# One 128-row bias load from a 128-copy table in place of two 64-row loads from a 64-copy table

## The chip, the cores and the metric

The kernel runs on one core of one Trainium2 chip. The metric is the device time of that core in microseconds. Three runs of the kernel before gave 2240.4, 2241.33 and 2242.48 us; their median is 2241.33 us. The lower the time, the better.

The engines have these names here: PE is TensorE, DVE VectorE, ACT ScalarE, POOL GpSimd, SP SyncE. PE multiplies, DVE and ACT prepare operands and post-process, POOL does small elementwise work and issues some DMAs, SP issues the weight loads.

## The reference

The program is a small transformer stack on 256 tokens with model width 1024. Two mixer layers come first; each adds to x the output projection of three gated attention branches. Then come four layers of a second block (sliding-window, gated-linear, forgetting and again sliding-window attention, each with a SwiGLU). All is float32. The part that matters here is the relative-position bias of two of the three branches of a mixer layer:

```
bias = bias_tab[t5_bucket(kpos[None, :] - qpos[:, None])]        # diff_attention, 8 heads
s = einsum('bqmhd,bkmhd->bmhqk', qblk, k) * scale + bias

bias = bias_tab[t5_bucket(delta * r)]                            # dilated_group, 3 groups of 4 heads
s = einsum('bnqhd,bnkhd->bnhqk', qs, kb) * scale + bias
s = where(valid, s, NEG_INF)
```

The bias of a query q and a key k depends on the head and on k - q alone. There are 8 + 12 = 20 heads with such a bias, and the kernel folds the mask of the dilated groups into it. Both mixer layers use the same table.

## The kernel before

**Weights.** Every weight matrix is streamed from HBM in pieces of 256 rows by 512 columns (512 KB, one DMA or two of 256 KB) into eight buffers `raw`. SP issues these loads (`h_piece`); a buffer is loaded again when DVE has read its last piece. A piece is then split into a rounded part `whi` (ACT, L144) and a rest `wlo` (DVE, L150), of which there are seven buffers each, and PE multiplies three times: high by high, high by low, low by high (L138). Some pieces (`in_ada_w`) are not multiplied on PE but reduced on DVE into a block of the tile `pool` (L155, then L158).

**Order of the work.** Every engine's program is recorded by one planner, which walks the network once and sends each step to the engine that owns it. Engines run their lists in order and wait for each other by semaphores. Small steps are placed by `soon`, a list that counts GEMM steps down; the attention heads are placed between weight pieces by estimated costs. The planner's estimates have no term for the bias loads or for the writes of the table.

**The bias.** Early on (`table`, L1077 on) one small matmul and one DVE addition (`h_btab`) make a block `btb` of 20 rows by 512 columns: row h holds the bias of head h as a function of k - q, for -255 to 256. To turn such a row into a tile in which partition q holds the row shifted by q, it is copied through HBM. `write_scratch(k)`, k = 0 to 3, is called 4, 7, 10 and 13 steps after the start of the first GEMM; each call issues one DMA on POOL's queue that writes every row of `btb` 16 times into the HBM tensor `bias_scratch`, which so holds 64 copies of each row. When the four writes have landed, `btb`'s two blocks of `pool` are free again; the next to use them is DVE's accumulation of an `in_ada_w` piece.

`get_bias(u)` is called for each attention unit: once per head of the differential branch, and for three heads of a dilated unit. It takes one of six buffers `bias_t` [128, 384] and issues, on POOL's queue, two DMAs (`h_bias`): partitions 0 to 63 and partitions 64 to 127. The source steps 511 elements from one partition to the next in copies that are 512 long, so that each partition starts one element earlier; the second half starts 64 elements earlier in the first copy. Both wait for the four writes and for the buffer's last reader. The reader is DVE's L158 `S<-A,bias_t` (`h_dil` and `h_diff`, step "max"), which adds the scaled logits in PSUM to the bias. In all there are 20 such tiles in each of the two mixer layers.

**POOL's list.** Beside these it holds the write and the reading back of one layer's memory keys and values (`kv_scratch`), and the small powers of the norms (`sm<-sm,mhalf`, L150), one of 128x1 or 128x2.

Of the kernel before, what the change touches and what calls it, by code (L numbers as in the profile page):

```python
# [7 lines left out]
F32 = mybir.dt.float32  # L8
# [5 lines left out]
P = 128  # L14
# [74 lines left out]
class Tally:  # L89
# [3 lines left out]
    def __init__(self, nc, ctx):  # L93
        self.nc, self.ctx, self.sem, self.n, self.value, self.real = nc, ctx, {}, {}, {}, False
# [164 lines left out]
class Memory:  # L259


    def __init__(self, nc, ctx, I, C, out):
        def sb(name, shape, dt=F32):
            return ctx.enter_context(nc.sbuf_tensor(name, shape, dt))

        self.I, self.C, self.out = I, C, out
        self.raw = sb("raw", [P, NRAW, 2, 512])
        self.whi = sb("whi", [P, NSPL, 2, 512], F32R)
        self.wlo = sb("wlo", [P, NSPL, 2, 512], F32R)
        self.X = sb("X", [P, 2, D])  # L270
        self.HTh, self.HTl = sb("HTh", [P, 8, T], F32R), sb("HTl", [P, 8, T], F32R)
        self.OTh, self.OTl = sb("OTh", [P, 8, T], F32R), sb("OTl", [P, 8, T], F32R)
        self.pool = sb("pool", [P, NB, 256])
        self.bias_t = sb("bias_t", [P, 6, 384])
        self.ident = sb("ident_t", [P, P])
        self.identr, self.maskr = sb("identr", [P, P], F32R), sb("maskr", [P, 256], F32R)
        self.cols = sb("cols", [P, 80])
        self.adb = sb("adb", [P, 192])
        self.mod = sb("mod", [P, 256])
        self.sm = sb("sm", [P, SM])  # L280
        self.c8 = sb("c8", [P, 8])
        self.ones = sb("ones", [P, 1])
        self.mhalf = sb("mhalf", [P, 16])
        self.nlam = sb("nlam", [P, 2])
        self.rmem = sb("rmem", [P, 2])
        self.w16 = sb("w16", [P, 256], F32R)
        self.w16h, self.w16l = (self.w16[:, 128 * i:128 * i + 128].rearrange("p (c n) -> p c n", n=16) for i in range(2))
        self.sel = sb("sel", [P, 16], F32R)
        self.S = [sb(f"S{j}", [P, 1040]) for j in range(2)]
        self.W = [sb(f"W{j}", [P, 1536]) for j in range(2)]  # L290
        self.GB = [ctx.enter_context(nc.psum_tensor(f"G{i}", [P, 512], F32)) for i in range(4)]
        self.AB = [ctx.enter_context(nc.psum_tensor(f"A{i}", [P, 2, 512], F32)) for i in range(2)]
        self.kvs = nc.dram_tensor("kv_scratch", (2, P, D), F32, kind="Internal").ap()
        self.mrows = nc.dram_tensor("mod_rows", (4, 64, P), F32, kind="Internal").ap()
        self.scratch = nc.dram_tensor("bias_scratch", (20, 64, 512), F32, kind="Internal").ap()


def cseg(w, r0, nk, segs):
# [128 lines left out]
class Order:  # L427
# [661 lines left out]

    def write_scratch(self, k):  # L1090

        self.scr.append(self.load("POOL", f"scr{k}", self.M.scratch[:, 16 * k:16 * k + 16, :],
                                  self.btb.a[0:20, :].unsqueeze(1).to_broadcast([20, 16, 512]), [self.tbt, self.step]))
        if k == 3:
            self.btb.release(self.scr)

    def get_bias(self, u):
        u["bias"] = []
        for i, h in enumerate([u["h"]] if u.kind == "diff" else [8 + gi * 4 + u["h"] for gi in range(3)]):
            r = self.bias_at.pop(0)  # L1100
            evs = [(f"bias{r}", (u.name, i, k)) for k in range(2)]
            for k in range(2):
                src = bass.AP(self.M.scratch.tensor, h * 64 * 512 + 127 - 64 * k, [[511, 64], [1, 384]])
                self.h_bias(r, 64 * k, src, self.scr, self.bias_free[r], evs[k])
            u["bias"].append((r, evs[1]))

    def biased(self, u):

# [2089 lines left out]
class GpSimdE(Order):  # L3198
# [26 lines left out]
        e.wait_ge(*self.at(prev))  # L3225
        e.tensor_tensor(m, m, gq, ALU.add).then_inc(*self.up(added))

    def h_bias(self, r, p, src, scr, free, ev):
        e = self.e
        for t in scr + free:  # L3230
            e.wait_ge(*self.at(t))
        e.dma_start(self.M.bias_t[p:p + 64, r, :], src).then_inc(*self.up(ev, 16))

    def h_rope(self, ps, t, dst, nh, tmp, cb, full, trp, free, read, done):
        e = self.e
# [79 lines left out]
```

## Time and profile before

| | |
|---|---|
| Median of the runs | 2241.33 us (2240.4 to 2242.48) |
| Time of the profiled execution | 2242.48 us |
| Span in its trace | 2240.7 us |
| PE busy / weight loads on PE | 2158.3 us (96%) / 1926.5 us (86%) |
| DVE / ACT / POOL busy | 1565.2 / 1029.2 / 206.1 us |
| Bytes moved | 472.98 MB, of these 29.61 MB on POOL's queue |

A span is the time from the first to the last instruction of the trace; the profiled execution's own time is 1.8 us longer. Busy time of PE says how long it had a matmul under way. The chain that ended last is followed back from the last instruction, at each step to whatever released it; what is not on it did not set the end in this execution. A timeline row shows a start, a duration, an instruction and, in brackets, how long the engine was idle before and what ended that. A DMA has two times: the issue, during which POOL is occupied, and the landing, counted from the start of the issue.

### The profile page before, as it was taken

How to read it: one execution, taken by the hardware profiler on the slowest of the kernel's cores; microseconds unless marked ns; L12 is line 12 of the kernel's file. 1: busy time of each engine (PE TensorE's matmuls, PEld its weight loads, DVE VectorE, ACT ScalarE, POOL GpSimd, SP SyncE). 2: the span in 40 equal slices, each digit the busy share in tenths (PEclk: the TensorE clock that was granted, in tenths of full speed). 3: DMA queues.
4: the chain of work that ended last, by engine and by line, in shares of the span. 5: the costliest groups of instructions: out<-in, count | busy, mean ns of one | idle time of the engine just before them, and what ended most of it. 6: DMA issues, size and time to landing. Idle time of an engine off the chain costs nothing.

```text
span 2240.7 us, 34043 instructions
## 1 busy us (share of the span) xinstructions
PE 2158.3 (96%) x13827; PEld 1926.5 (86%) x13827; DVE 1565.2 (70%) x2153; ACT 1029.2 (46%) x1698; POOL 206.1 (9%) x244
## 2 busy tenths in 40 slices
PE   7999999999999999999999998999999999999996
PEld 6999888889998888777999787999898899788996
DVE  6577657766676677667898677899645895667454
ACT  5444445544444564455434544444455443454342
POOL 1101001101010011010001001001000001111010
PEclk9999999999999999999999999999999999999998
DMA  8977645577786455534899434799544797425551
GB/s 303 290 249 218 226 156 161 168 235 225 240 266 199 135 165 200 190 122 143 301 343 343 155 107 141 262 358 357 186 132 141 262 355 247 148 94 187 189 181 64
DMA packets 297425, 472.98 MB, mean 211 GB/s; under 512 B 20257, under 2 KB 153067, under 8 KB 297269
## 3 DMA queue, kind: packets, MB, share of 16 engines
q1 hardware_dynamic: 286708, 441.20, 58.4%
q0 software_dynamic: 10560, 29.61, 4.4%
q8 instruction: 109, 1.79, 0.3%
q14 instruction: 48, 0.39, 0.1%
HBM read 465.88 MB, written 4.85 MB: 210 GB/s over the span
## 4 chain that ended last, share of the span: by engine, by line
PE 88%; DVE 6%; issue 2%; ACT 2%; POOL 1%; DMA 1%; SPq 0%; DVEq 0%; POOLq 0%; ACTq 0%
PE G L138 69%; PE A L138 16%; PE G L141 2%; DVE pool L158 2%; DVE wlo L150 1%; DVE pool L150 1%; POOL sm L150 1%; ACT pool L144 1%; DVE X L150 1%; PE A L141 1%; DVE HTl L158 0%; DMA raw<-in_w_mem_kv 0%; ACT HTh L144 0%; DVE sm L155 0%; DMA pool<-mod_rows 0%
## 5 line engine op out<-in xcount | busy, mean ns | idle before, releaser
L150 DVE TENSOR_TENSOR wlo<-raw,whi 128x1024 fp32r<-128x1024 f32 x640 | 772.7, 1235 | 181.2 <-ACT whi L144 179.5
L144 ACT ACTIVATE whi<-raw 128x1024 fp32r<-128x1024 f32 x640 | 646.5, 1054 | 192.9 <-DMA raw<-in_ffn_w_gu 94.8
L138 PE MATMUL G<-HTh,whi 128*128 128x256 f32 x2336 | 672.8, 288 | 9.6 <-ACT pool L144 4.8
L138 PE MATMUL G<-HTh,wlo 128*128 128x256 f32 x2336 | 662.3, 284 | 0.0
L138 PE MATMUL G<-HTl,whi 128*128 128x256 f32 x2336 | 662.2, 283 | 0.0
L138 PEld LDWEIGHTS G<-HTh,whi 128*128 128x128 f32 x2336 | 449.3, 192 | 17.9 <-DVE wlo L150 9.4
L138 PEld LDWEIGHTS G<-HTl,whi 128*128 128x128 f32 x2336 | 449.5, 192 | 2.1
L138 PEld LDWEIGHTS G<-HTh,wlo 128*128 128x128 f32 x2336 | 449.1, 192 | 0.0
L144 ACT ACTIVATE pool<-G 128x512 f32<-128x512 f32 (+2 forms) x208 | 115.5, 573 | 537.9 <-PE G L138 503.8
L138 PE MATMUL G<-whi,HTh 128*128 128x512 f32 (+1 forms) x784 | 313.4, 400 | 14.9 <-ACT HTh L144 9.3
L138 PE MATMUL G<-whi,HTl 128*128 128x512 f32 (+1 forms) x784 | 304.2, 388 | 4.3 <-DVE HTl L158 4.1
L138 PE MATMUL G<-wlo,HTh 128*128 128x512 f32 (+1 forms) x784 | 301.9, 385 | 0.0
L158 DVE SCALAR_TENSOR_TENSOR pool<-raw,c,pool 128x512 f32<-128x512 f32 x336 | 267.7, 797 | 7.4
L158 DVE SCALAR_TENSOR_TENSOR pool<-pool,G 128x512 f32<-128x512 f32 (+1 forms) x140 | 91.7, 656 | 173.3 <-ACT pool L144 141.8
L138 PEld LDWEIGHTS G<-whi,HTh 128*128 128x128 f32 x784 | 149.4, 191 | 50.9 <-issue 9.1
L138 PEld LDWEIGHTS G<-whi,HTl 128*128 128x128 f32 x784 | 148.9, 190 | 43.2 <-DVE HTl L158 13.9
L138 PEld LDWEIGHTS G<-wlo,HTh 128*128 128x128 f32 x784 | 149.4, 191 | 25.3
L138 PE MATMUL A<-whi,OTh 128*128 128x512 f32 x352 | 138.6, 394 | 0.0
L138 PE MATMUL A<-wlo,OTh 128*128 128x512 f32 x352 | 137.3, 390 | 0.0
L138 PE MATMUL A<-whi,OTl 128*128 128x512 f32 x352 | 137.1, 390 | 0.0
L138 PE MATMUL G<-whi,OTh 128*128 128x512 f32 x272 | 109.2, 402 | 0.9 <-DVE HTl L158 0.9
L150 POOL TENSOR_TENSOR sm<-sm,mhalf 128x1 f32<-128x1 f32 (+1 forms) x44 | 51.0, 1159 | 635.9 <-DVE sm L155 635.9
(195 smaller groups left out, 2314.4 us busy)
## 6 DMA issues: line engine op xcount, KB each, us to landing
raw<-in_ada_w SPq DMA_DIRECT2D x192, 512.0 KB, 5.9
raw<-in_ffn_w_gu SPq DMA_DIRECT2D x352, 256.0 KB, 5.0
raw<-in_w_in SPq DMA_DIRECT2D x128, 512.0 KB, 4.6
raw<-in_ffn_w_down SPq DMA_DIRECT2D x88, 512.0 KB, 6.7
raw<-in_w_in SPq DMA_DIRECT2D x160, 256.0 KB, 4.7
raw<-in_swa_w_in SPq DMA_DIRECT2D x24, 512.0 KB, 5.5
pool<-mod_rows POOLq DMA_DIRECT2D x24, 512.0 KB, 6.3
raw<-in_gla_w_in SPq DMA_DIRECT2D x24, 512.0 KB, 5.0
```

The source lines that it names most:

```text
L138: return self.e.matmul(out, a, b, start=start, stop=stop, skip_group_check=True) if self.e else self
L141: return self.e.transpose(out, a, ident) if self.e else self
L144: return self.e.activation(out, a, func, bias=bias, scale=scale, accum_out=accum) if self.e else self
L150: return self.e.tensor_tensor(out, a, b, op) if self.e else self
L158: return self.e.scalar_tensor_tensor(out=out, in0=a, scalar=s, in1=b, op0=op0, op1=op1) if self.e else self
```

## The change

The table in HBM now has 128 copies of each row (`bias_scratch` is 20 x 128 x 512). Each of the four writes carries 32 copies instead of 16, so 1280 KB instead of 640 KB. A bias tile is filled by one DMA of 128 partitions instead of two of 64; the bytes of a tile are the same. `h_bias` has one argument less, and there is one semaphore event per tile instead of two. Nothing else is touched.

```diff
@@ -292,7 +292,7 @@
         self.AB = [ctx.enter_context(nc.psum_tensor(f"A{i}", [P, 2, 512], F32)) for i in range(2)]
         self.kvs = nc.dram_tensor("kv_scratch", (2, P, D), F32, kind="Internal").ap()
         self.mrows = nc.dram_tensor("mod_rows", (4, 64, P), F32, kind="Internal").ap()
-        self.scratch = nc.dram_tensor("bias_scratch", (20, 64, 512), F32, kind="Internal").ap()
+        self.scratch = nc.dram_tensor("bias_scratch", (20, P, 512), F32, kind="Internal").ap()
 
 
 def cseg(w, r0, nk, segs):
@@ -1089,8 +1089,8 @@
 
     def write_scratch(self, k):
 
-        self.scr.append(self.load("POOL", f"scr{k}", self.M.scratch[:, 16 * k:16 * k + 16, :],
-                                  self.btb.a[0:20, :].unsqueeze(1).to_broadcast([20, 16, 512]), [self.tbt, self.step]))
+        self.scr.append(self.load("POOL", f"scr{k}", self.M.scratch[:, 32 * k:32 * k + 32, :],
+                                  self.btb.a[0:20, :].unsqueeze(1).to_broadcast([20, 32, 512]), [self.tbt, self.step]))
         if k == 3:
             self.btb.release(self.scr)
 
@@ -1098,11 +1098,10 @@
         u["bias"] = []
         for i, h in enumerate([u["h"]] if u.kind == "diff" else [8 + gi * 4 + u["h"] for gi in range(3)]):
             r = self.bias_at.pop(0)
-            evs = [(f"bias{r}", (u.name, i, k)) for k in range(2)]
-            for k in range(2):
-                src = bass.AP(self.M.scratch.tensor, h * 64 * 512 + 127 - 64 * k, [[511, 64], [1, 384]])
-                self.h_bias(r, 64 * k, src, self.scr, self.bias_free[r], evs[k])
-            u["bias"].append((r, evs[1]))
+            src = bass.AP(self.M.scratch.tensor, h * P * 512 + 127, [[511, P], [1, 384]])
+            ev = (f"bias{r}", (u.name, i))
+            self.h_bias(r, src, self.scr, self.bias_free[r], ev)
+            u["bias"].append((r, ev))
 
     def biased(self, u):
 
@@ -3225,11 +3224,11 @@
         e.wait_ge(*self.at(prev))
         e.tensor_tensor(m, m, gq, ALU.add).then_inc(*self.up(added))
 
-    def h_bias(self, r, p, src, scr, free, ev):
+    def h_bias(self, r, src, scr, free, ev):
         e = self.e
         for t in scr + free:
             e.wait_ge(*self.at(t))
-        e.dma_start(self.M.bias_t[p:p + 64, r, :], src).then_inc(*self.up(ev, 16))
+        e.dma_start(self.M.bias_t[:, r, :], src).then_inc(*self.up(ev, 16))
 
     def h_rope(self, ps, t, dst, nh, tmp, cb, full, trp, free, read, done):
         e = self.e
```

The lists of PE, ACT and SP and that of DVE hold the same instructions in the same order. POOL's list is the one that changes. First its start, around the writes of the table and the first loads (the difference, with - for before and + for the change; `rmem`, `sm` and `mhalf` are small tiles of the norms):

```order
 L150 TENSOR_TENSOR rmem<-sm,mhalf 128x1 x2
-L170 DMA bias_scratch<-pool 20x16x512 x2
+L170 DMA bias_scratch<-pool 20x32x512 x2
 L150 TENSOR_TENSOR sm<-sm,mhalf 128x1 x2
-L170 DMA bias_scratch<-pool 20x16x512 x2
+L170 DMA bias_scratch<-pool 20x32x512 x2
 L170 DMA kv_scratch<-pool 128x1024 x2
-L170 DMA bias_t<-bias_scratch 64x384 x30
+L170 DMA bias_t<-bias_scratch 128x384 x15
 L150 TENSOR_TENSOR sm<-sm,mhalf 128x2
```

The writes stand where they stood, twice as large, and behind them 15 loads take the place of 30. Then the end of a mixer layer, where the loads of the differential heads alternate with the powers:

```order
-L170 DMA bias_t<-bias_scratch 64x384 x4
+L170 DMA bias_t<-bias_scratch 128x384 x2
 L150 TENSOR_TENSOR sm<-sm,mhalf 128x2
-L170 DMA bias_t<-bias_scratch 64x384 x2
+L170 DMA bias_t<-bias_scratch 128x384
 L150 TENSOR_TENSOR sm<-sm,mhalf 128x2
-L170 DMA bias_t<-bias_scratch 64x384 x2
+L170 DMA bias_t<-bias_scratch 128x384
 L150 TENSOR_TENSOR sm<-sm,mhalf 128x2 x2
```

No power changes its place among the loads. Last, the place on DVE that waits for the four writes (`s_scr0` to `s_scr3` are their semaphores, `s_raw7` that of the weight buffer); it reads the same before and in the change:

```order
L150 TENSOR_TENSOR wlo<-raw,whi 128x1024 [waits s_ac_hi] x10
L158 SCALAR_TENSOR_TENSOR pool<-raw,c8,pool 128x512 [waits s_ve_ada,s_raw5]
L158 SCALAR_TENSOR_TENSOR pool<-raw,c8,pool 128x512 [waits s_ve_ada]
L150 TENSOR_TENSOR wlo<-raw,whi 128x1024 [waits s_ac_hi]
L155 TENSOR_SCALAR pool<-raw,c8 128x512 [waits s_scr2,s_scr1,s_scr3,s_scr0,s_raw7]
L158 SCALAR_TENSOR_TENSOR pool<-raw,c8,pool 128x512 [waits s_ve_ada]
L150 TENSOR_TENSOR wlo<-raw,whi 128x1024 [waits s_ac_hi]
```

Nothing moved here; the TENSOR_SCALAR is the first instruction of DVE that reuses the table's blocks. The other waits for what stands on POOL's queue are ACT's: its 128x512 copies `pool<-G` into the blocks of `kv_scratch`'s source.

## Rows read from the trace of the kernel before

**Rows 1.** The page: its head, and the shares of the chain that ended last by engine
```profile
span 2240.7 us, 34043 instructions
...
PE 88%; DVE 6%; issue 2%; ACT 2%; POOL 1%; DMA 1%; SPq 0%; DVEq 0%; POOLq 0%; ACTq 0%
```
**Rows 2.** The page's DMA issues: tiles, count, KB each, median us to landing
```profile
bias_t<-bias_scratch POOLq DMA_DIRECT2D x80, 96.0 KB, 4.7
...
bias_scratch<-pool POOLq DMA_DIRECT2D x4, 640.0 KB, 8.1
```
**Rows 3.** Instructions on tile bias_t, 0 to 900 us: ns min/median/max, first and last start
```profile
L170 POOL DMA_DIRECT2D bias_t<-bias_scratch x80: 516/526/688, 75.5 to 825.6; - x80
L158 DVE SCALAR_TENSOR_TENSOR S<-A,bias_t x80: 411/424/693, 171.9 to 844.7; 128x256 f32<-128x256 f32 x48, 128x512 f32<-128x512 f32 x32
...
  DMA bias_t<-bias_scratch: 1.1, 2
...
DMA to landing us min/median/max: 2.2/4.7/8.0
```
**Rows 4.** The chain in order of time, 60 to 900 us: its shares, one piece
```profile
by line: PE G L138 83.1%; PE A L138 8.6%; PE G L141 1.9%; DVE wlo L150 1.2%; PE A L141 1.0%; DVE S L158 0.7%; ACT pool L144 0.7%; DVE S L155 0.6%; DVE sm L161 0.6%; issue 0.5%; DVE sm L155 0.3%; ACT HTh L144 0.2%; DVE pool L158 0.2%; DVE mo
...
801.24 5.66 PE G L138 x24
```
**Rows 5.** Timeline of POOL: start us, us, instruction, idle before and what ended it
```profile
48.38 0.56 POOL L150 TENSOR_TENSOR sm<-sm,mhalf 128x1 f32<-128x1 f32 x1 [4.24 <-DVE sm L155]
...
64.56 0.70 POOL L170 DMA_DIRECT2D bias_scratch<-pool  x1 [10.23 <-PE G L138]
65.25 0.60 POOL L170 DMA_DIRECT2D kv_scratch<-pool  x1
...
75.52 6.21 POOL L170 DMA_DIRECT2D bias_t<-bias_scratch  x12 [1.35 <-DMA bias_scratch<-pool]
...
795.65 1.59 POOL L150 TENSOR_TENSOR sm<-sm,mhalf 128x2 f32<-128x2 f32 x1 [21.50 <-DVE sm L155]
797.19 2.09 POOL L170 DMA_DIRECT2D bias_t<-bias_scratch  x4
...
823.49 1.61 POOL L150 TENSOR_TENSOR sm<-sm,mhalf 128x2 f32<-128x2 f32 x1 [19.15 <-DVE sm L155]
```
**Rows 6.** Timeline of DVE, at three places
```profile
90.91 0.48 DVE L155 TENSOR_SCALAR pool<-raw,c 128x512 f32<-128x512 f32 x1
...
96.92 1.23 DVE L150 TENSOR_TENSOR wlo<-raw,whi 128x1024 fp32r<-128x1024 f32 x1 [4.74 <-ACT whi L144]
...
803.42 1.29 DVE L158 SCALAR_TENSOR_TENSOR S<-A,bias_t 128x512 f32<-128x512 f32 x2 [0.91 <-DMA bias_t<-bias_scratch]
```
**Rows 7.** Two stretches: engines' busy us, PEclk, DMA share of 16 engines, GB/s
```profile
34.00:62.00 28.00, 26.95 (x180) 24.27 (x179) 20.95 (x28) 17.09 (x27) 3.49 (x5) 1.00 0.79 240
62.00:97.00 35.00, 35.00 (x210) 31.31 (x209) 16.16 (x18) 14.71 (x19) 8.06 (x15) 1.00 1.01 333
```
**Rows 8.** DMA of 35 to 42 us: POOL's queue, packets, MB, share of 16; its issue
```profile
q0 software_dynamic: 272, 0.66, 33.6%
...
bias_scratch<-pool POOLq DMA_DIRECT2D x1, 640.0 KB, 6.9
```
**Rows 9.** POOL's queue alone, 39 to 40 us
```profile
q0 software_dynamic: 37, 0.15, 64.0%
```
**Rows 10.** DMA issues under way at 64 to 77 us (the fourth write)
```profile
bias_scratch<-pool POOLq DMA_DIRECT2D x1, 640.0 KB, 10.4
```
**Rows 11.** DMA issues of 76.3 to 76.8 us (one weight load)
```profile
raw<-in_w_in SPq DMA_DIRECT2D x1, 512.0 KB, 14.4
```
**Rows 12.** Timeline of ACT, 95 to 108 us
```profile
95.82 3.90 ACT L144 ACTIVATE whi<-raw 128x1024 fp32r<-128x1024 f32 x4
106.37 1.09 ACT L144 ACTIVATE pool<-G 128x512 f32<-128x512 f32 x2 [6.65 <-PE G L138]
```
**Rows 13.** Instructions on tile whi, 62 to 110 us: TensorE's token-stationary form
```profile
L138 PE MATMUL G<-HTh,whi x72: 277/283/283, 83.1 to 108.7; 128*128 128x256 f32 x72
```

## The prediction, made before the changed kernel was run

> **What bounds the kernel now.** I read the page first: the chain that ended last is 88% PE, and POOL and DMA have 1% each [rows 1]. Then I looked for where the changed operations stand. The DMA issues give 80 loads of bias tiles and 4 writes of the table [rows 2]. The view by tile says who waits for them: in 80 uses DVE waited twice for a load, 1.1 us together, and POOL spends 526 ns on an issue [rows 3]. The chain from 60 to 900 us, the stretch with all bias work, names PE for over nine tenths and has neither POOL nor a DMA of the bias [rows 4]. So the change works on two things off the path, POOL's queue and the DMA engines, and the question is whether the larger writes can push their way onto it. They are made while the DMA engines are most loaded: their mean share is 0.79 from 34 to 62 us and 1.01 from 62 to 97 us [rows 7]. (The share is of packets in flight, so that it can pass 1.)
>
> **The loads, halved in number.** POOL now issues 80 x 0.526 = 42.1 us [rows 3]. An issue for 128 partitions of 1.5 KB isn't in the trace; it lies between the 0.526 us of a half and the 0.60 us of the kv_scratch write, which has 128 partitions [rows 5]. I take 0.60: 40 x 0.60 = 24.0 us, so POOL gets 18.1 us back. Were they all on the path, they would be worth 18.1 us; I take 0, because POOL's loads are followed by a power which waits for DVE anyway (19.15 us idle before the one at 823.49) [rows 5] and the chain does not pass through POOL there [rows 4].
>
> What is left of the loads is their landing. The bytes of a tile are the same. The last of the four at 797.19 [rows 5] isn't the one that DVE waits for; it waits for the first pair, 0.91 us until 803.42 [rows 6]. One DMA instead of a pair is issued complete about 0.5 us sooner, so this wait should fall to some 0.4 us, and the other (1.1 - 0.91 = 0.2 us) should vanish. From both sides: all of 1.1 us gained at best; at worst a load of twice the rows lands a median of 4.7 us later [rows 3] at both places, 9.4 us. PE stands in 24 matmuls without a gap from 801.24 to 806.90 [rows 4], over the wait and beyond it, so I take 0.
>
> The Trainium skill (DMA: Bandwidth & Descriptors, section Rules for kernel authors) says that two transfers to disjoint partition halves share the same engines and should be one 128-partition transfer. By that the landing gain is real, and the trace says that at most 1.1 us of it could be used: the sum would be 1.1 us lower.
>
> **The writes, doubled.** One write occupied POOL's queue for 33.6% of 16 engines over 7 us, 0.336 x 16 x 7 = 37.6 us of engine time, 272 packets with 0.66 MB [rows 8]. Four times as much again is 150 us of engine time, or 9.4 us of all 16 engines. How late do weights land by it? Between 34 and 62 us there is room: (1.01 - 0.79) x 28 = 6.2 us of all engines [rows 7], and the first three writes add 3 x 2.35 = 7.1 us. That leaves 0.9 us; the fourth write, issued at 64.56 [rows 5] in the full stretch, adds 2.35 us. Weights that land after 65 us are about 3.2 us later. That is my value; the ends are 0 (all absorbed) and the landing times passed on one to one, 6.9 + 8.1 + 8.1 + 10.4 = 33.5 us [rows 2, 8, 10].
>
> What lateness can PE stand? The tightest piece is one whose load is issued at 76.4 and lands 14.4 us later, at 90.8 [rows 11]. It is the first of the four that ACT splits from 95.82 [rows 12]; DVE starts its rest at 96.92 and ends at 98.15 [rows 6], 2.3 us after ACT's start. PE works through nine pieces from 83.1 to 108.7, 8 of the 72 triples each [rows 13]; by the order of the splits this one is the eighth, so that PE comes to it 56/71 of the way, at 83.1 + 20.2 = 103.3. It may land at 101.0 at the latest, 10.2 us later than it does. 3.2 us are well inside, and even 9.4 us with nothing absorbed are. Price: 0.
>
> The other readers of the writes have more room. DVE's TENSOR_SCALAR at 90.91 [rows 6] needs all four landed; the last landed at 64.56 + 10.4 = 75.0 [rows 5, 10]. If its landing doubles to 20.8 us it is 85.4, still 5.5 us early, and DVE then has 4.74 us idle before 96.92 [rows 6]. The first loads start when the writes have landed, at 75.52 [rows 5]; 10.4 us later they start at 85.9, and the slowest landed in 8.0 us [rows 3], by 100 at the latest with their 6.21 us of issues, against a first use at 171.9 [rows 3]. The kv_scratch writes stand behind the fourth write, and ACT needs the first of them at 106.37 [rows 12], over 40 us after its issue at 65.25 [rows 5]. POOL's issue of a write grows too: 0.70 us for 320 rows against 0.526 for 64 [rows 3, 5] is 0.7 ns a row, so 320 more rows add 0.2 us; the power at 48.38 waits 4.24 us for DVE anyway [rows 5].
>
> A write seems to run on ten engines, not sixteen: its queue's share in the middle of the first write is 64.0%, 10.2 of 16 [rows 9]. A weight load spreads over all and lands with its slowest part, so 37.6 us on ten engines are 3.8 us instead of 2.35, and the lateness is 3.2 x 1.6 = 5.1 us, still half of 10.2. The Trainium skill gives the rule (DMA: Bandwidth & Descriptors, section Why a DMA increments its semaphore by 16 and not by 1): the engine count is the largest divisor, up to 16, of both slowest dimensions, which for 20 rows is ten. The trace agrees with its 64.0%. It speaks against the change, but by it too the sum gains nothing.
>
> **Sum.** The profiled execution took 2242.48 us, its span 2240.7 [rows 1] and 1.8 around it. Loads 0 (at best -1.1), writes 0: 2242.5 by that execution, which was the slowest of three and 1.15 us over their median. For a median I put it at 2241.5 us.
>
> **Rival A, slower: the writes hold the weights back.** If the last two writes pass their extra landing on in full (8.1 + 10.4 = 18.5 us), the piece above is 18.5 - 10.2 = 8.3 us too late and PE stands: 2249.8 us. The point from which it decides is 10.2 us of lateness. For it: the full stretch, the ten engines (with nothing absorbed and always the same ten, 150/10 = 15.0 us, so 4.8 us lost, 2246.3). Against it: the write shares the engines with weight loads, whose queue has the larger part, and the 28 us before have room. At the very end, 33.5 - 10.2 = 23.3 us lost, 2264.8.
>
> **Rival B, slower at the loads.** The 128-row load lands 4.7 us later at both places where DVE waits, and nothing hides it: 2241.5 + 9.4 = 2250.9. Against it: same bytes, and pairs queue behind each other today.
>
> **Rival C, faster: POOL's powers get shorter.** The power at 823.49, which follows loads, takes 1.61 us while the one at 48.38 takes 0.56 [rows 5]. Were the loads the cause, six such powers in the two layers would save 1.05 each, 6.3 us: 2235.2. Against it: the one at 795.65 takes 1.59 though it follows no load directly, and none is on the chain from 60 to 900 us [rows 4, 5].
>
> **Rival D: the change doesn't do what it says**, the DMA splitting one 128-row load as before. Then nothing moves either, and the time is the forecast's.
>
> **Chances.** A measurement of this kernel can tell about 0.2% (4.5 us) from no change. The forecast with D 0.87; A 0.05; B and the like 0.03; C and gains at the landing beyond what I see 0.05. So faster 0.05, same 0.87, slower 0.08. The range: the three runs lie within 1.2 us of their median; downward the 1.1 us of waits are added, upward some leaked lateness, up to 4 us. I give 2239.0 to 2245.5; it leaves out A, B and C.
>
> **What would show it.** Right: POOL has 40 bias loads and about 18 us less to do; DVE's wait for bias loads under 1 us; the writes with 1.3 MB each on POOL's queue and the DMA share from 34 to 62 us nearer to 1; ACT's splits around 87 and 96 us waiting up to a few us for a weight load, PE without a gap until 109 us. Wrong: PE idle on `wlo` between 61 and 110 us, the TENSOR_SCALAR at 91 us waiting for the table, or a DVE wait for `bias_t` that grows and shows on the chain.

## The result and the profile after

The change made the kernel slower: 2252.81 us median (2249.95 to 2257.41, four runs) against 2241.11 us (2240.4 to 2242.48, four runs), a ratio of 1.0053 with a 95% interval of 1.0036 to 1.0072. The prediction was 2241.5 us and gave "slower" 8%. The profiled execution took 2250.89 us. Its page's head and chain, which answer to [rows 1]:

```profile
span 2249.1 us, 34003 instructions
...
PE 2157.9 (96%) x13827; PEld 1924.6 (86%) x13827; DVE 1565.4 (70%) x2153; ACT 1028.9 (46%) x1698; POOL 187.7 (8%) x204
...
PE 87%; DVE 6%; issue 2%; ACT 2%; DMA 1%; POOL 1%; SPq 1%; DVEq 0%; POOLq 0%; ACTq 0%
```

No engine has more to do, POOL has 18.4 us less (206.1 before), and the span is 8.4 us longer. The order of the instructions is the same on PE, DVE, ACT and SP, so the start of each of PE's 13,827 matmuls can be set against its own start before. The difference stands at -0.9 us at 60 us, at +10.7 at 84 us and at +11.4 at the last matmul. So the whole loss, 11.6 us, is made between 60 and 84 us. The windows show the same place; the columns are those of [rows 7]:

```profile
34.00:62.00 28.00, 26.94 (x180) 24.25 (x179) 21.64 (x29) 16.51 (x26) 3.74 (x5) 1.00 0.93 242
62.00:97.00 35.00, 26.93 (x118) 21.86 (x117) 9.82 (x9) 10.22 (x13) 5.17 (x9) 0.85 0.96 282
```

From 34 to 62 us the DMA share rose from 0.79 to 0.93 and the rate stayed: 242 GB/s against 240 [rows 7]. The engines were held longer and moved no more. From 62 to 97 us PE lost 8.1 of its 35 us, and its granted clock is 0.85 in the mean, a mix of the levels 2.4 and 1.2 GHz, where it was 1.00.

What stood in the way is in the DMA issues of 30 to 100 us (tiles, count, KB each, median us to landing):

```profile
bias_scratch<-pool POOLq DMA_DIRECT2D x4, 1280.0 KB, 18.9
raw<-in_w_in SPq DMA_DIRECT2D x8, 512.0 KB, 16.8
raw<-in_w_in SPq DMA_DIRECT2D x12, 256.0 KB, 11.9
```

The writes, issued at 33.83, 42.57, 52.76 and 63.73, landed after 13.9, 18.1, 19.7 and 20.7 us; before it was 6.9 to 10.4 [rows 8, 10]. Beside them the weights of `in_w_in` took 11.9 (256 KB) and 16.8 us (512 KB) in the median; in the same view of before it is 5.0 and 12.4 us. SP's issues grew too. First its run of 14 issues in this place before, then the same 14 now:

```profile
46.43 19.08 SPq L170 DMA_DIRECT2D raw<-in_w_in  x14
```

```profile
45.58 37.97 SPq L170 DMA_DIRECT2D raw<-in_w_in  x14
```

A run also holds SP's waits for a free buffer. By the trace's records the issues alone make up 10.3 of the 19.08 us before and 35.3 of the 37.97 now.

ACT splits each weight piece when it has landed. Four pieces that it split in a row before, without a wait,

```profile
61.42 4.00 ACT L144 ACTIVATE whi<-raw 128x1024 fp32r<-128x1024 f32 x4
```

now come one by one, the wait in brackets:

```profile
61.30 1.06 ACT L144 ACTIVATE whi<-raw 128x1024 fp32r<-128x1024 f32 x1 [0.60 <-DMA raw<-in_w_in]
63.17 1.06 ACT L144 ACTIVATE whi<-raw 128x1024 fp32r<-128x1024 f32 x1 [0.81 <-DMA raw<-in_w_in]
73.55 1.06 ACT L144 ACTIVATE whi<-raw 128x1024 fp32r<-128x1024 f32 x1 [9.32 <-DMA raw<-in_w_in]
81.67 1.06 ACT L144 ACTIVATE whi<-raw 128x1024 fp32r<-128x1024 f32 x1 [7.07 <-DMA raw<-in_w_in]
```

And the chain that ended last, which had no DMA here, goes through SP's blocked issues, the load and the fourth split:

```profile
61.13 2.88 SPq L170
64.02 0.04 issue
64.06 17.59 DMA raw<-in_w_in
81.65 0.02 issue
81.67 1.07 ACT whi L144
82.74 0.02 issue
82.76 1.24 DVE wlo L150
84.00 0.04 issue
84.04 35.86 PE G L138 x246
```

The load of the fourth piece was issued at 56.63 and landed at 63.12 before; now it was issued at 64.06 and landed at 81.65. So of the 18.5 us by which it landed later, 7.4 are a later issue and 11.1 a longer landing.

The matmul that takes up the third piece began at 74.98 before and at 75.92 now. The one that takes up the fourth began at 76.34 and now at 84.04, right behind DVE's rest:

```profile
76.34 0.39 PE L138 MATMUL G<-whi,HTh 128*128 128x512 f32 x1
```

```profile
75.92 0.50 PE L138 MATMUL G<-whi,HTh 128*128 128x512 f32 x1 [1.61 <-DVE wlo L150]
84.04 0.80 PE L138 MATMUL G<-whi,HTh 128*128 128x512 f32 x1 [6.46 <-DVE wlo L150]
```

With the 0.9 us by which this execution was ahead, that is 1.8 and 8.6 us. After that hardly a wait is left, but the difference grows by another 3.0 us until 84 us (in the time of before). PE had stood from 77.6 to 84.0 us, and from 84 to 90 us its granted clock is 0.50, the lower level of 1.2 GHz:

```profile
84.00:90.00 6.00, 5.96 (x14) 4.70 (x15) 2.17 (x2) 2.62 (x3) 3.77 (x7) 0.50 0.93 313
```

From 90 to 97 us it is 0.99. So the loss is 8.6 us of standing and 3.0 us of slow clock.

The span grew by 8.4 us and not by 11.4, since the program also ends sooner behind PE's last matmul. The last rows of DVE, before and now:

```profile
2229.94 1.41 DVE L158 SCALAR_TENSOR_TENSOR pool<-X,sm,pool 128x512 f32<-128x512 f32 x2 [0.67 <-POOL sm L150]
```

```profile
2241.37 1.41 DVE L158 SCALAR_TENSOR_TENSOR pool<-X,sm,pool 128x512 f32<-128x512 f32 x2 [0.67 <-POOL sm L150]
```

From there to the end of the span it is 9.4 us before and 6.3 us now. The raw record names what ends last: an instruction of POOL called DRAIN, 11.14 us long before and 8.12 us now; behind it come only the engines' last semaphore signals, within 0.2 us. The bias loads show nothing else: DVE's wait for `bias_t` (1.1 us [rows 3]) is gone.

### The profile page after: what moved, and what is told of

Read it like the earlier page. It is cut to its first block, busy times and chain, and to the rows that moved or that the text cites. A ratio compares the mean times of both kernels' runs of the same rounds, so it can differ in the third digit from the quotient of the medians.

```text
span 2249.1 us, 34003 instructions
## 1 busy us (share of the span) xinstructions
PE 2157.9 (96%) x13827; PEld 1924.6 (86%) x13827; DVE 1565.4 (70%) x2153; ACT 1028.9 (46%) x1698; POOL 187.7 (8%) x204
## 3 DMA queue, kind: packets, MB, share of 16 engines
q0 software_dynamic: 10304, 32.23, 5.0%
## 4 chain that ended last, share of the span: by engine, by line
PE 87%; DVE 6%; issue 2%; ACT 2%; DMA 1%; POOL 1%; SPq 1%; DVEq 0%; POOLq 0%; ACTq 0%
PE G L138 69%; PE A L138 16%; PE G L141 2%; DVE pool L158 2%; DVE wlo L150 1%; DVE pool L150 1%; POOL sm L150 1%; ACT pool L144 1%; DVE X L150 1%; PE A L141 1%; DMA raw<-in_w_in 1%; SPq L170 1%; DVE HTl L158 0%; DMA raw<-in_w_mem_kv 0%; ACT HTh L144 0%
## 5 line engine op out<-in xcount | busy, mean ns | idle before, releaser
L144 ACT ACTIVATE whi<-raw 128x1024 fp32r<-128x1024 f32 x640 | 647.2, 1055 | 222.2 <-DMA raw<-in_ffn_w_gu 92.8
L138 PEld LDWEIGHTS G<-HTh,whi 128*128 128x128 f32 x2336 | 448.3, 192 | 17.9 <-DVE wlo L150 8.5
L138 PEld LDWEIGHTS G<-whi,HTl 128*128 128x128 f32 x784 | 149.2, 190 | 43.6 <-DVE HTl L158 13.9
L138 PE MATMUL G<-whi,OTl 128*128 128x512 f32 x272 | 106.2, 390 | 0.0
```

The lines of the kernel that those rows point to most:

```text
L138: return self.e.matmul(out, a, b, start=start, stop=stop, skip_group_check=True) if self.e else self
L144: return self.e.activation(out, a, func, bias=bias, scale=scale, accum_out=accum) if self.e else self
```

## The experiments

Twelve runs gave a time, in four lots of three, four, four and one, each lot on a chip of its own. A thirteenth, e_load, was to have the loads of the change without its writes and gave no result; e_load64 stands for it. Each ratio is to runs of the kernel before on the same chip at the same time (their median was 2242.6 to 2244.2 us, beside the change 2241.1). "Loss on PE" is the difference of the start of the same matmul at 189 us, less that at 60 us, as above: +11.6 for the change. "Drain" is POOL's last DRAIN. For e_first2 and e_last2 the landings are those of the table's own four writes. The last three columns are worked out from the traces' records; the sections below say what each run is.

| run | us | ratio, 95% | writes land after, us | loss on PE | drain |
|---|---|---|---|---|---|
| the change | 2252.81 | 1.0053 [1.0036, 1.0072] | 13.9 18.1 19.7 20.7 | 11.6 | 8.12 |
| e_write | 2255.66 | 1.0057 [1.0042, 1.0072] | 14.4 20.2 21.4 22.5 | 12.6 | 11.14 |
| e_load64 | 2239.79 | 0.9984 [0.9975, 0.9994] | 7.4 8.3 8.8 9.5 | 0.0 | 4.68 |
| e_ports | 2241.23 | 0.9993 [0.9983, 1.0002] | 11.9 14.8 13.0 13.6 | 0.0 | 8.11 |
| e_spread | 2241.35 | 0.9995 [0.9986, 1.0005] | 8.3 8.6 9.0 11.3 | 0.0 | 8.28 |
| e_rows16 | 2263.39 | 1.0093 [1.0077, 1.0110] | 15.6 20.9 23.9 20.1 | 21.3 | 8.28 |
| e_pitch | 2251.37 | 1.0035 [1.0022, 1.0048] | 14.6 17.9 19.4 20.1 | 11.8 | 8.11 |
| e_late | 2256.92 | 1.0063 [1.0046, 1.0080] | 12.8 16.5 20.8 23.0 | 14.9 | 8.03 |
| e_first2 | 2250.85 | 1.0033 [1.0020, 1.0047] | 11.8 15.7 13.8 10.3 | 6.6 | 11.13 |
| e_last2 | 2248.31 | 1.0018 [1.0009, 1.0028] | 7.3 8.2 11.4 15.5 | 5.3 | 11.14 |
| b_spread | 2244.71 | 1.0005 [0.9995, 1.0014] | 6.1 6.8 6.4 7.9 | 0.0 | 11.14 |
| b_short | 2238.39 | 0.9974 [0.9964, 0.9985] | 4.4 6.1 5.3 6.5 | 0.0 | 6.16 |
| e_half20 | 2239.54 | 0.9982 [0.9972, 0.9991] | 4.8 5.8 5.3 5.6 | 0.0 | 6.56 |

### Which half of the change: the writes

The cuts of code below are shortened, with ... for what is left out. **e_write** keeps the two loads of 64 rows and takes only the table of 128 copies.

```
-        self.scratch = nc.dram_tensor("bias_scratch", (20, 64, 512), ...
+        self.scratch = nc.dram_tensor("bias_scratch", (20, P, 512), ...
-        self.scr.append(self.load("POOL", f"scr{k}", self.M.scratch[:, 16 * k:16 * k + 16, :],
-                                  self.btb.a[0:20, :].unsqueeze(1).to_broadcast([20, 16, 512]), ...
+        self.scr.append(self.load("POOL", f"scr{k}", self.M.scratch[:, 32 * k:32 * k + 32, :],
+                                  self.btb.a[0:20, :].unsqueeze(1).to_broadcast([20, 32, 512]), ...
```

> The write part alone: the table has 128 copies and each write 1280 KB, as in the change, but each bias tile is still filled by two 64-row loads. Theory W (the doubled writes cost the time, by delaying weight loads between 34 and 87 us): the whole loss is here, 2251 to 2255 us, with the writes landing after 14 to 21 us and ACT waiting some 16 us for weights between 62 and 82 us. Rival L (the 128-row loads cost it, in issue or landing): 2241 us as before.

**e_load64** is the other half: one load of 128 rows from a table of 64 copies.

```
+            src = bass.AP(self.M.scratch.tensor, h * 64 * 512 + 63, [[64, 2], [511, 64], [1, 384]])
```

> The load part alone: the table keeps its 64 copies (640 KB a write, as before), and each bias tile is filled by one load of 128 rows that reads the 64 copies twice (rows 64 to 127 get the shift of rows 0 to 63, so half of the biases are other ones than the reference's). Theory W (the write part has the whole loss): 2241 +- 1.5 us, ratio to before 0.999 to 1.0008; the four writes land after 7 to 10.5 us as before, and PE stays busy 25.0 of the 25 us from 62 to 87. POOL does about 15 us less work and that gives nothing. Theory L (the load of 128 rows takes part in the loss): over 2244 us, with DVE's add waiting for the bias load.

The writes alone lose 12.6 us on PE (and 2255.66 us is 0.7 over the range written), the loads alone nothing up to 189 us. The ratio of e_load64 is even under 1 and under the 0.999 written, and the table says where it is from: at POOL's drain, 6.5 us shorter than before. This isn't free. The loads of this form land in a median of 10.3 us from 60 us on instead of 4.7, and DVE waits:

```profile
DVE S L158 <- DMA bias_t<-bias_scratch: 10.0, 2, 5.0
```

That is about the 9.4 us of lateness of Rival B, and it cost 3.3 us at most: matmuls start 2.6 us later than before at 1090 us, where they had been 0.7 early at 801.

### What in the writes: where their source rows lie

Three things about a write of 20 rows could hold up others: it runs on ten engines (theory E), its source rows are neighbouring partitions (theory P), its 20 streams stand at a pitch of a power of two in HBM (theory H).

**e_ports** writes the same 20 rows in 32 copies each, from partitions 26, 29, ... 83. For that the table is computed in 100 partitions, five times the 20 rows; the 20 partitions taken hold each head once, in another order, and the loads follow that order.

```
-    self.btb.a[0:20, :].unsqueeze(1).to_broadcast([20, 32, 512])
+    self.btb.a[26:84:3, :].unsqueeze(1).to_broadcast([20, 32, 512])
```

> The change, but the 20 rows that a write reads lie in partitions 26, 29, ..., 83 instead of 0 to 19; bytes, rows, number of DMA engines (ten) and the table's layout in HBM stay. Theory P (the write is slow because its 20 source partitions lie side by side, so that ten engines read through a few paths of SBUF: 160 packets took 4 us before, some 16 GB/s an engine, where a weight load moves 24 GB/s an engine): the writes land in 8 to 11 us instead of 14 to 21, and the time is 2241 to 2246 us. The Trainium skill (SBUF, State Buffer, section Door 1) says that groups of four neighbouring partitions share one of 16 ports; 20 neighbours would be five ports. Theory E (ten engines carry all of it and are simply full): nothing moves, 2251 to 2255 us. Theory H (the layout in HBM is what is slow): nothing moves either.

**e_spread** computes the table in 80 partitions and writes 8 copies from each, over sixteen engines.

```
-   self.M.scratch[:, 32 * k:32 * k + 32, :],
-   self.btb.a[0:20, :].unsqueeze(1).to_broadcast([20, 32, 512])
+   bass.AP(self.M.scratch.tensor, 8 * k * 80 * 512, [[512, 80], [80 * 512, 8], [1, 512]]),
+   self.btb.a[0:80, :].unsqueeze(1).to_broadcast([80, 8, 512])
```

> The change with the same bytes, but a write reads 80 partitions (four replicas of the 20 rows, made by the same matmul) and writes 8 copies of each, so that it can use 16 engines; the table is stored copy by copy, so that heads lie 2 KB apart. Theory E: an engine carries 82 KB instead of 131 KB per write and weights are late by 5/8 of 12 to 18 us at most; 2241 to 2246 us. Theory P: 80 partitions spread too, 2241 to 2244 us. Theory H: the layout changed, 2241 to 2244 us. If it stays at 2251 to 2255 us, bytes alone decide and all three are wrong.

**e_rows16** keeps the bytes of a write and takes 16 rows of 40 copies, partitions 0 to 15.

```
-    self.btb.a[0:20, :].unsqueeze(1).to_broadcast([20, 32, 512])
+    self.btb.a[0:16, :].unsqueeze(1).to_broadcast([16, 40, 512])
```

> The change with the same 1280 KB in each write, but as 16 rows of 40 copies instead of 20 rows of 32: the source rows are partitions 0 to 15, so the write goes over all sixteen engines, from 16 neighbouring partitions. Heads 16 to 19 read the tables of heads 12 to 15, so their biases are other ones than the reference's. Theory E (the loss is that only ten engines carry the write): recovers, 2241 to 2243 us, writes land after 9 to 12 us. Theory P (the loss is that the source rows lie in neighbouring partitions, which share few ports): stays slow, 2250 us or more, writes land after 14 to 22 us, weight loads beside them late on all sixteen engines, PE busy 15 to 20 of the 25 us from 62 to 87.

**e_pitch** puts the tables of two heads 133 copies apart.

```
+        self.scratch = nc.dram_tensor("bias_scratch", (20, P + 5, 512), ...
```

> The change with the tables of two heads 133 instead of 128 copies apart in HBM, so that the 20 heads' rows of one write no longer lie 256 KB apart. Theory H (twenty streams at a pitch of a power of two meet in HBM): recovers toward 2241 to 2245 us, writes land after 9 to 13 us. Theory P (source partitions share few ports) and theory E (ten engines): no difference from the change, 2250 to 2256 us, ratio to before 1.004 to 1.007, writes land after 14 to 21 us.

e_ports and e_rows16 part E from P, and both go P's way. With ten engines, but other partitions, the loss is gone (e_ports). With sixteen engines, but sixteen neighbours, it nearly doubles (e_rows16). Pitch changes nothing (e_pitch; its ratio, 1.0035, is just under the 1.004 written).

The ten engines aren't free even so. The writes of e_ports landed after 11.9 to 14.8 us, not the 8 to 11 that theory P gave, and the third and fourth weight piece landed 6.3 and 5.0 us later than before, not counting the 1.0 us by which this execution was behind at 60 us already. That stays within the 8.7 and 9.0 us that PE can stand, worked out in the section on why the prediction was wrong. The windows 34:62 and 62:87 of e_ports:

```profile
34.00:62.00 28.00, 27.21 (x185) 24.55 (x183) 21.58 (x29) 16.07 (x26) 3.90 (x5) 1.00 0.90 291
62.00:87.00 25.00, 24.73 (x121) 21.01 (x122) 11.18 (x11) 11.88 (x16) 5.17 (x9) 1.00 1.01 369
```

and of e_rows16:

```profile
34.00:62.00 28.00, 25.29 (x172) 22.82 (x170) 18.27 (x25) 11.72 (x19) 3.03 (x5) 1.00 1.00 184
62.00:87.00 25.00, 15.87 (x60) 11.88 (x60) 6.19 (x6) 6.18 (x8) 1.25 (x2) 0.85 1.02 168
```

At a share of 1.00 the sixteen engines moved 184 GB/s, at 0.90 they moved 291. The share says how long engines are held, not what they carry. What the writes do is read from POOL's queue alone, here from 36 to 46 us (packets, MB, share of 16 engines); first e_rows16, then the change, e_ports and e_spread:

```profile
q0 software_dynamic: 253, 1.04, 92.8%
```

```profile
q0 software_dynamic: 529, 1.34, 55.7%
```

```profile
q0 software_dynamic: 523, 1.30, 34.9%
```

```profile
q0 software_dynamic: 336, 1.31, 36.6%
```

From 16 neighbours it is 104 GB/s. The other three moved the same bytes, 130 to 134 GB/s in the mean of these ten us, but the change's writes hold the engines 1.5 times as long for them (55.7% against 34.9 and 36.6%). In the midst of a write the rates part as well: 41 to 44 us of e_rows16, the change and e_ports, and 39 to 42 us of e_spread, whose write ends at 43.8:

```profile
q0 software_dynamic: 78, 0.32, 95.0%
```

```profile
q0 software_dynamic: 99, 0.41, 62.8%
```

```profile
q0 software_dynamic: 167, 0.68, 58.9%
```

```profile
q0 software_dynamic: 250, 1.02, 94.2%
```

That is 107, 137, 227 and 340 GB/s. The change and e_ports both fill about ten of 16 engines, and the spread rows get 1.7 times the bytes through them. In e_rows16 the write stands on all sixteen engines, and the 256 KB loads of `in_w_in` issued from 34 to 62 us land in a median of 24.8 us; in the change it is 12.4 and in e_ports 8.1.

The Trainium skill (SBUF — State Buffer, section Door 1: The DMA port swizzle) says that DMA bandwidth depends on how many of 16 ports the partitions reach, and that four neighbours share one. By its table partitions 0 to 19 reach five ports, 0 to 15 four, the 20 of e_ports thirteen and 80 rows twelve. By the 435 GB/s that the page gives for all 16, five ports would carry an estimated 136 GB/s and four 109; the trace agrees in the midst of a write with 137 and 107. At the start of the first write it doesn't: from 37 to 40 us the change moved 0.60 MB, 200 GB/s, and why stays open. It is a rule that I had not weighed. The one that I had, of the ten engines, holds too, but e_ports shows that it alone costs PE nothing.

### When it happens: not in one place alone

**e_late** issues the change's four writes some 20 steps later.

```
-  enumerate((4, 7, 10, 13))
+  enumerate((24, 27, 30, 33))
```

> The change with its four 1280 KB writes (still 20 neighbouring partitions) issued about 20 steps later, so at some 100 to 130 us instead of 34 to 64, after the stretch in which PE ran out of weights. Theory S (the loss is made where the writes meet the weight loads that have the least slack, those that ACT needs from 61 us on): recovers, 2238 to 2243 us, PE busy about 25 of the 25 us from 62 to 87, although each write still takes 10 to 18 us. Rival (a write that holds up the weights costs the same wherever it stands): 2248 to 2255 us, with PE idle behind the late writes.

**e_first2** and **e_last2** add a write of 640 KB to the kernel before, behind its first two or its last two.

```
+        if k in (0, 1):      # e_last2: (2, 3)
+            self.load("POOL", f"more{k}", self.M.more[:, 16 * k:16 * k + 16, :],
+                      self.btb.a[0:20, :].unsqueeze(1).to_broadcast([20, 16, 512]), ...)
```

> The kernel before with one more write of 640 KB from the same 20 partitions (to a table of its own that nobody reads) behind each of the first two writes, at about 34 and 42.6 us, so that the first two carry the change's 1280 KB and the last two the 640 KB of before. Theory S (what counts is the backlog at 50 to 64 us): the backlog of the first two is mostly gone by then; 2240 to 2244 us, the four writes of the table land after 7 to 13 us. Rival (every write of the four has its share): half of the loss, 2245 to 2248 us.

> The kernel before with one more write of 640 KB behind each of the last two writes, at about 52.8 and 63.7 us. Theory S (what counts is the backlog at 50 to 64 us): most of the loss, 2246 to 2255 us, with ACT waiting for raw<-in_w_in behind 64 us and PE busy under 20 of the 25 us from 62 to 87. Rival (every write has its share): 2245 to 2248 us. If the first two alone made the loss: 2241 us.

My theory S, that only the pieces with little slack around 61 us make the loss, fell: by the time in e_late and e_first2, by the busy time of PE in e_last2. In e_late the stretch from 62 to 87 us has its 25.00 us of PE back, and 14.9 us are lost behind the late writes. Its windows and its longest wait for weights from 30 to 180 us:

```profile
62.00:87.00 25.00, 25.00 (x129) 21.42 (x128) 10.99 (x11) 11.72 (x15) 2.03 (x3) 1.00 0.83 255
...
110.00:140.00 30.00, 15.60 (x111) 15.13 (x110) 12.29 (x22) 8.00 (x16) 3.27 (x6) 0.77 0.90 235
```

```profile
ACT whi L144 <- DMA raw<-in_w_in: 26.6, 6, 12.0
```

(Its first write left at 72.67, earlier than I had written, the others at 91.80, 100.45 and 109.08.) With the first two writes doubled 6.6 us are lost, at a piece of `in_w_mem_kv` already, whose load of 42.31 landed at 65.28:

```profile
ACT whi L144 <- DMA raw<-in_w_mem_kv: 8.5, 1, 8.5
```

With the last two doubled 5.3 us are lost. So every pair can make a loss. That 6.6 and 5.3 make 11.9, about the change's 11.6, may be chance: they are lost at other pieces. In the change that load of `in_w_mem_kv` landed at 54.1, and nothing was lost until 74 us. S gave 2240 to 2244 us for e_first2, and it took 2250.85. For e_last2 S gave PE under 20 of the 25 us from 62 to 87; it had 23.54. The time of 2248.31 would do for either theory, but the kernel before was at 2244.15 in this lot; the ratio of 1.0018 is 4 us, the lower end of the rival's range. In none of the three is the rival refuted, but its sizes were too small: e_late is over its range of 2248 to 2255 us by 1.9 us, e_first2 over its 2245 to 2248 by 2.9 and e_last2 by 0.3, with the kernel before 3 us higher in this lot than I had reckoned.

### Versions that are worth having

**b_spread** spreads the source of the kernel before over 80 partitions (640 KB a write).

> The kernel before (64 copies, two loads of 64 rows for each tile) with the table computed in 80 partitions (four times the 20 heads), so that each write of 640 KB leaves from 80 partitions over sixteen engines. Theory P: writes land after 5 to 8 us instead of 7 to 10.4, the weights beside them earlier; but PE is busy 25.00 of 25 us there in the kernel before, so the time is the same: 2240.5 us +- 1.2, ratio 0.9988 to 1.0003. Rival (the writes of before still hold PE somewhere, late weights behind 87 us): up to 3 us faster, 2238 us.

The writes land sooner, after 6.1 to 7.9 us, and nothing is gained: PE had its 25.00 us before. This was as theory P said; the time, 2244.71 us, is over the range written, with the kernel before at 2243.45 beside it.

**b_short** has only 24 copies. Row p of a tile reads 127 - p elements into some copy, it doesn't matter which; inside groups of 16 rows the load steps from copy to copy (511), and from the start of one group to the start of the next it goes one copy on and 16 elements back (496 = 512 - 16).

```
-        self.scratch = nc.dram_tensor("bias_scratch", (20, 64, 512), ...
+        self.scratch = nc.dram_tensor("bias_scratch", (20, 24, 512), ...
+   self.M.scratch[:, 6 * k:6 * k + 6, :] <- self.btb.a[0:20, :] to [20, 6, 512]
+            src = bass.AP(self.M.scratch.tensor, h * 24 * 512 + 127, [[496, 8], [511, 16], [1, 384]])
```

> A table of 24 copies instead of 64 or 128 (240 KB a write), and one load of 128 rows for each bias tile that steps from one copy to the next inside groups of 16 rows; all biases are those of the reference. Theory P and S: the writes land after 4 to 6 us and nothing holds the weights; PE is busy 25.0 of 25 us from 62 to 87 as before, so no more than the end of POOL's queue is to be had: its last drain took 11.1 us in the kernels with 80 bias loads, 8.1 to 8.3 in those with 40, and 4.7 with the 64-copy loads of 128 rows. With 4.7 to 8.3 us here the time is 2234 to 2240 us, ratio 0.997 to 1.000. Rival: that the loads break up into smaller packets makes DVE wait for biases and eats it, 2240 to 2243 us.

**e_half20** keeps the two loads of 64 rows and has 20 copies.

> The kernel before, with its two loads of 64 rows for each bias tile kept (80 in all), and a table of 20 copies instead of 64 (200 KB a write, a seventh of the change's; the loads step from copy to copy inside groups of 16 rows). It parts the two gains of the table of 24 copies. If the number of bias loads sets POOL's last drain: it takes 11.1 us as in the other kernels with 80 loads, and the time is 2239 to 2241.5 us in a lot where before is at 2241 (ratio 0.9985 to 1.0000). If how the loads read the table sets it: a drain of 5 to 9 us and a ratio of 0.997 to 0.999. If the small writes themselves were worth something on PE, PE's matmuls from 84 us on would start over 1 us earlier than in the table of 24 copies; theory P and S say that they don't.

b_short took 2238.39 us, ratio 0.9974 (0.9964 to 0.9985), faster than both kernels and within what was written. Nothing of it is PE's: the loss on PE is 0.0, as in every run with writes that spread or shrink. The gain is at the end, where POOL's drain is 5.0 us shorter; the profiled spans differ by 6.0 (1.0 of it lies in the first 32 us, before any changed instruction). e_half20 has 80 loads and a drain of 6.56 us, so the number of loads does not set it, against the first of its theories. It goes with how the loads read the table: 11.1 us in all five kernels with plain loads of 64 rows, 8.0 to 8.3 in all six with plain loads of 128, 4.7 to 6.6 in the three that step through the table. What POOL does in its drain, and why these forms differ, stays open. It isn't the packets of its queue (10,560 before and the same in b_short).

## Why the prediction was wrong, by its steps

**The loads: right, their number in part by luck.** POOL's busy time fell by 18.4 us (18.1 forecast), DVE's wait went, and neither is on the path. An issue for 128 rows takes 3.20/6 = 0.53 us, not the 0.60 I took, so the issues of the loads alone fell by 21.1 us (42.95 to 21.88 by the trace's records); longer issues of the writes and 1.1 us more of POOL's elementwise work `OTl<-pool,OTh` took part of that back.

**"Between 34 and 62 us there is room: (1.01 - 0.79) x 28 = 6.2 us of all engines": this step failed.** It took a mean share of engine time as room that the writes could fill at no cost to the weights. Of that room nothing was had: the rate in the stretch stayed at 242 GB/s, the writes got 3.10 of its MB (1.97 before) and the weights 3.64 (4.72 before). It isn't the ten engines alone: e_ports, on ten as well, moved 291 GB/s here, with 3.47 MB of writes and 4.66 MB of weights. It is the rate at which 20 neighbouring rows leave, 137 GB/s in the midst of a write, by which 1280 KB take an estimated 9.6 us with nothing else there. Nor does twice the bytes mean twice the engine time: POOL's queue held 25.1% of the 16 engines for its 1.97 MB and 54.2% for its 3.10, which is 57 and 78 us of engine time per MB.

**The lateness, 3.2 us (5.1 by ten engines): mis-sized, the term that decides.** The third piece of the four landed 13 us later than before (73.5 against 60.45) and the fourth 18.5 us later (81.65 against 63.12). Rival A's 15.0 us (ten engines, nothing absorbed) and 18.5 (extra landing passed on in full) were the terms near it. The writes landed 7.0, 10.0, 11.6 and 10.3 us later; the fourth piece's 18.5 us are 7.4 of a later issue on SP and 11.1 of a longer landing. For a later issue the prediction had no term, so that Rival A's figure being the same is chance. Working with engine time (37.6 us spread over 16) hid all of it.

**The slack, 10.2 us: the wrong piece.** I took a load with a long landing (14.4 us), split at 95.82; it wasn't even the longest, since the one issued at 67.41 took 19.7 us. The pieces split from 61.42 had less: DVE's rest of the fourth was ready at 67.39 and PE took it up at 76.34, 9.0 us of slack; the third had 8.7. With 17.5 us of lateness (83.99 against 67.39, and the 0.9 us of head start) PE stands 17.5 - 9.0 = 8.5 us, the 8.6 measured. The piece with the least slack in the chain from load to use has to be looked for among all; one long landing is not the sign. Of the two sizes the lateness decides: 3.2 us are inside 9.0 as well, and 17.5 are over 10.2 as well.

**No term for the clock.** PE's standing brought the lower clock, 3.0 us more. **No term for the end** of the program, where 3.0 us were won. These two cancel.

**The other readers: right.** The fourth write landed at 84.4 (85.4 forecast), the loads of biases started at 85.02 (85.9), a write's issue takes 0.14 us more (0.2).

**Rival A was the case**, by its mechanism; its price, 2249.8 us, came near the 2252.81 by luck, by a sum on another piece with no clock in it. Rival B's cost was not seen in the change. Rival C's powers did not shorten the kernel, and D was not so. What was wrong in the chances is that Rival A got 5%, though by its own working it decides once ten engines carry the writes (which a row showed) and nothing is absorbed, and no row said that something would be.

## What to carry to other kernels

A broadcast write from a few neighbouring partitions is slow at its source and holds the DMA engines all that time. Doubled here, its landing grew by 7 to 12 us, and two pieces of weights beside it landed 13 and 18.5 us later. Before a transfer is grown in a stretch where weights stream, look at GB/s beside the DMA share (high share at a low rate is no room), spread its source rows over the partitions, or make the table smaller. Then look for the least slack among all pieces between the transfer and their use, and add the clock that PE loses when it stands.

## What was not expected of the hardware

- POOL's queue held sixteen engines at 92.8% and moved 104 GB/s from 16 neighbouring partitions, while 20 rows from spread partitions on ten engines moved up to 227 GB/s (41 to 44 us) and cost PE nothing.
- SP's own issues took longer beside the writes: the same 14 took 35.3 us together instead of 10.3, and 15.5 in e_ports, where the writes leave from spread partitions.
- The end of the program waits for a DRAIN of POOL that takes 4.7 to 11.1 us. Its length goes with the form of the loads that POOL issued 1400 us earlier (the last bias load before was at 825 us, the DRAIN begins at 2229); why stays open.
- A load of 128 rows that reads 64 copies twice ([[64, 2], [511, 64], [1, 384]]) makes more than twice the packets on POOL's queue (21,440 against 10,304 in the whole kernel) and lands in 10.3 us instead of 4.7; the stepped one of b_short (10,560) lands in 6.0.
